# A gated delta rule core: inverse by transposes, modulation sums moved from TensorE to VectorE, pieces reordered

## What is computed

```python
a_mat = jnp.where(strict, bc[..., :, None] * kk * decay, 0.0) + jnp.eye(CHUNK)
rhs = jnp.concatenate([vc * bc[..., None], kc * (bc * jnp.exp(gam))[..., None]], axis=-1)
sol = lax.linalg.triangular_solve(a_mat, rhs, left_side=True, lower=True, unit_diagonal=True)
...
mod = (c_act @ ada_w[l] + ada_b[l])[:, None, :]
sh1, sc1, g1, sh2, sc2, g2 = jnp.split(mod, 6, axis=-1)
...
x = x + g1 * hybrid_mixer(h, ...)
```

## Time and profile before

| What | us |
| --- | --- |
| median of the runs | 2159.68 |
| span of the profiled execution | 2156.4 |
| the rest of that time, taken as median less span | 3.3 |
| TensorE busy | 1983.0 (92%) |
| VectorE busy | 511.2 (24%) |
| ScalarE busy | 327.1 (15%) |
| GpSimd busy | 96.9 (4%) |

### The profile page before, as it was taken

The page is one execution under the profiler, slowest core; times in us unless marked ns, Lnnn a source line. Parts: engine busy times, 40 slices in busy tenths (PEclk is TensorE's granted clock), DMA queues, the critical chain, the costliest instruction groups (busy, mean ns, idle before and its releaser), DMA issues. The chain is left out here.

```text
span 2156.4 us, 23922 instructions
## 1 busy us (share of the span) xinstructions
PE 1983.0 (92%) x9874; PEld 954.2 (44%) x9874; DVE 511.2 (24%) x1030; ACT 327.1 (15%) x572; POOL 96.9 (4%) x178
## 2 busy tenths in 40 slices
PE   6989999989999999999999999899999887777777
PEld 4677676643333333333333333355454432223322
DVE  2255453431222122121122111231342300000000
ACT  2133421220000000000000000213341200000001
POOL 2010052000000000000000000100030000000000
PEclk9999999999999999999999999999999998999999
DMA  9332254579999999999999999934243799999996
GB/s 342 117 122 84 73 210 173 206 312 425 428 428 429 429 428 428 428 428 429 428 429 428 429 429 429 394 119 168 63 152 155 287 428 429 428 429 429 428 429 290
DMA packets 98563, 707.10 MB, mean 328 GB/s; under 512 B 12314, under 2 KB 17932, under 8 KB 61516
## 3 DMA queue, kind: packets, MB, share of 16 engines
q1 hardware_dynamic: 98508, 706.36, 79.9%
HBM read 705.29 MB, written 1.05 MB: 328 GB/s over the span
## 5 line engine op out<-in xcount | busy, mean ns | idle before, releaser
L1674 PE MATMUL ps<-ring,arena 128*64 128x512 f32 x1536 | 337.5, 593 | 12.0 <-DMA ring<-in_moe_w_gu 12.0
L2870 PE MATMUL ps<-ring,arena 128*32 128x512 f32 x768 | 175.5, 621 | 41.5 <-DMA ring<-in_w_up 20.4
L1674 PEld LDWEIGHTS ps<-ring,arena 128*64 128x64 f32 x1536 | 109.8, 137 | 234.2 <-issue 206.1
L1701 PE MATMUL ps<-ring,arena 128*64 128x512 f32 x768 | 168.9, 592 | 0.0
L2107 PE MATMUL ps<-ring 128*128 128x512 f32 (+1 forms) x320 | 138.8, 583 | 0.7 <-ACT ring L2486 0.6
L1725 ACT ACTIVATE arena<-arena 128x512 f32<-128x512 f32 x32 | 20.2, 630 | 760.3 <-DVE arena L1756 760.3
L2870 PEld LDWEIGHTS ps<-ring,arena 128*32 128x32 f32 x768 | 52.8, 114 | 163.3 <-issue 161.4
L1674 PE MATMUL ps<-arena 128*64 128x512 f32 x512 | 113.5, 593 | 4.5 <-DMA arena<-in_moe_w_gu 4.5
L1069 PEld LDWEIGHTS ps<-arena 128*128 128x128 f32 x832 | 99.2, 197 | 35.3 <-issue 32.7
L1069 PE MATMUL ps<-arena 128*128 128x128 f32 x832 | 107.2, 285 | 2.3 <-DVE arena L1061 1.3
L1701 PEld LDWEIGHTS ps<-ring,arena 128*64 128x64 f32 x768 | 54.9, 137 | 109.9 <-issue 100.2
(11 more groups left out here) (581 smaller groups left out, 2093.5 us busy)
## 6 DMA issues: line engine op xcount, KB each, us to landing
ring<-in_moe_w_gu SPq DMA_DIRECT2D x96, 2048.0 KB, 28.8
ring<-in_moe_w_down SPq DMA_DIRECT2D x48, 2048.0 KB, 31.6
arena<-in_moe_w_gu SPq DMA_DIRECT2D x32, 2048.0 KB, 28.8
ring<-in_w_up SPq DMA_DIRECT2D x24, 2048.0 KB, 20.1
ring<-in_w_gate SPq DMA_DIRECT2D x24, 2048.0 KB, 26.9
ring<-in_w_down SPq DMA_DIRECT2D x24, 2048.0 KB, 27.0
ring<-in_w_in SPq DMA_DIRECT2D x22, 2048.0 KB, 8.4
arena<-in_moe_w_down SPq DMA_DIRECT2D x16, 2048.0 KB, 33.8
```

What stands on the lines that cost most here:

```text
L1674: last = M.matmul(ps[halves[j], 4 + which, :], xgT[buf][:, k, CAP * ee:CAP * ee + CAP], w[:, k2, at:at + 512], start=False, stop=(k == KD ...
L1701: last = M.matmul(ps[halves[j], 6, :], yT[:, k % KH, halves[k // KH]], w[:, k % KH, 512 * j:512 * j + 512], start=False, stop=(k == 2 * KH ...
L2870: last = M.matmul(ps[quads[e], 4 + which, :], xgT[:, k, quads[e]], w[e][:, k, :], start=(k == 0), stop=(k == KD - 1))
```

## The change

Three things are changed together, all within the 24 steps.

1. The product for Xi (Q1^T Xi) and its subtraction on VectorE are gone. In their place `transposed_back(i)` transposes the updated Yi on TensorE, and ScalarE copies it from PSUM over Xi (`take_transposed`). It comes in the program one step later, after `corrections(i+1)`, for i = 0 to 19; the last of these levels transposes 64 x 64 blocks only. `corrections(i)` now waits for the copy that belongs to step i-4, and each transpose waits for VectorE's update of Yi.
2. The late modulation sums no longer run on TensorE and ScalarE. VectorE forms them with 8 instructions for each of the 8 chunks, 128 x 512 each, which read the weights from the ring slot and one column of the condition as a scalar: one multiplication and seven multiply-adds, each waiting for the one before. Four such instructions follow the update in each of the steps 0 to 3 and three in each of the steps 4 to 19. `s_ada`, which frees the slot, is now raised by VectorE.
3. The pieces beside the steps have other places, and their waits are adapted.

```diff
+    LATE_SUMS = [(j, k) for j in range(4, 12) for k in range(KD)]
+    def late_sums_of(i):
+        at = 4 * i if i < 4 else 16 + 3 * (i - 4)
+        return LATE_SUMS[at:at + (4 if i < 4 else 3)]
...
-    BESIDE = {0: [("mt", 0)], 1: [("sum", 4)], 2: [("spread", 4), ("sum", 5)], 3: [("spread", 5)], 4: [("mt", 1)],
...
+    BESIDE = {0: [("mt", 0)], 1: [("mt", 1)], 2: [("spread", 4)], 4: [("spread", 5)], 5: [("out", 0, 0)], 6: [("out", 0, 1)],
+              7: [("spread", 6)], 8: [("out", 1, 0)], 10: [("spread", 7)], 11: [("out", 1, 1)], 12: [("spread", 8)],
+              15: [("spread", 9)], 18: [("spread", 10)], 20: [("spread", 11)]}
...
+                if i >= 4:
+                    pe.wait_ge(s_yt, 2 + i - 3)
                 for h in range(4 * g, 4 * g + 4):
...
-                if lv < NL - 1:
-                    for h in range(4 * g, 4 * g + 4):
-                        last = M.matmul(ps[:, 4 + i % 2, (h % 4) * P:(h % 4 + 1) * P], Q1[t][:, h, :], Xi[t][:, h, :])
                 last.then_inc(s_dd, 1)
+            def transposed_back(i):
+                lv, t, g = STEPS[i]
+                pe.wait_ge(s_upd, i + 1)
+                if i >= 2:
+                    pe.wait_ge(s_yt, 2 + i - 1)
+                for h in range(4 * g, 4 * g + 4):
+                    if lv < NL - 2:
+                        last = M.transpose(ps[:, 4 + i % 2, (h % 4) * P:(h % 4 + 1) * P], Yi[t][:, h, :], ident[:, :])
+                    else:
+                        last = M.transpose(ps[0:HB, 4 + i % 2, (h % 4) * HB:(h % 4 + 1) * HB], Yi[t][0:HB, h, 0:HB], ident[0:HB, 0:HB])
+                last.then_inc(s_xt, 1)
...
-                elif kind == "sum":
...
-                    modulation_sums(pe, cond, 6)
                 elif kind == "spread":
-                    pe.wait_ge(s_part, j + 1)
-                    if j > 4:
+                    pe.wait_ge(s_ada, j + 1)
+                    if j == 4:
+                        pe.wait_ge(s_mTt, 2)
+                    else:
                         pe.wait_ge(s_modt, j - 4)
...
                     if t == 0:
-                        chunk[n] = ra.take(pe)
+                        chunk[n] = ra.arrived(pe, out_chunk[1, n])
                     pe.wait_ge(s_mTt, 2)
-                    if n:
-                        pe.wait_ge(s_part, 8)
-                        pe.wait_ge(s_modt, 4)
+                    if n and t == 0:
+                        pe.wait_ge(s_wev, 1)
+                    if t:
+                        pe.wait_ge(s_modt, 4 if n else 2)
...
                 corrections(i)
+                if 1 <= i <= NSTEP - 4:
+                    transposed_back(i - 1)
                 for piece in BESIDE.get(i, ()):
                     beside(piece)
...
+            def take_transposed(i):
+                lv, t, g = STEPS[i]
+                act.wait_ge(s_xt, 2 + i + 1)
+                if lv < NL - 2:
+                    A.activation(Xi[t][:, 4 * g:4 * g + 4, :], four(4 + i % 2), ACT.Copy).then_inc(s_yt, 1)
...
-                    elif piece[0] == "sum":
-                        j = piece[1]
-                        act.wait_ge(s_ada, j + 1)
-                        act.wait_ge(s_comb, j - 1)
-                        A.activation(mod_parts[j % 2], ps[:, 6, :], ACT.Copy).then_inc(s_part, 1)
...
+            def late_sum(j, k):
+                acc = mod_parts[j % 2]
+                if k == 0:
+                    late_w[j] = ra.arrived(dve, late_chunk[j])
+                    dve.wait_ge(s_comb, j - 1)
+                    vv(V.tensor_scalar(acc, late_w[j][:, 0, :], cond[:, 0, 0:1], None, ALU.mult))
+                else:
+                    ins = V.scalar_tensor_tensor(acc, late_w[j][:, k, :], cond[:, k, 0:1], acc, ALU.mult, ALU.add)
+                    if k < KD - 1:
+                        vv(ins)
+                    else:
+                        ins.then_inc(s_ada, 1)
...
                 dve.wait_ge(s_dd, i + 1)
-                y, x = Yi[t][:, 4 * g:4 * g + 4, :], Xi[t][:, 4 * g:4 * g + 4, :]
+                y = Yi[t][:, 4 * g:4 * g + 4, :]
                 if lv < NL - 1:
-                    vv(V.tensor_tensor(x, x, four(4 + i % 2), ALU.subtract))
                     V.tensor_tensor(y, y, four(2 + i % 2), ALU.subtract).then_inc(s_upd, 1)
...
+                for j, k in late_sums_of(i):
+                    late_sum(j, k)
```

More of the change, by code:

```diff
@@ L185, in load, with arrived @@
                 self.sent += 1
+        def arrived(self, eng, n):
+            _, (k, w), _, s, arrivals, _ = self.chunks[n]
+            eng.wait_ge(self.full[s], arrivals)
+            return slot(s, k, w)
         def take(self, pe):
-            _, (k, w), _, s, arrivals, _ = self.chunks[self.used]
-            pe.wait_ge(self.full[s], arrivals)
             self.used += 1
-            return slot(s, k, w)
+            return self.arrived(pe, self.used - 1)
     w_in, ada_w = a["w_in"][0], a["ada_w"][0]
@@ L209, in program @@
     s_wout = sem("w_out_chunk_multiplied")
+    late_chunk, out_chunk = {}, {}
     def add_late(j, s):
+        late_chunk[j] = len(ra.chunks)
         ra.add(cols(ada_w, 512 * j), (KD, 512), (s_ada, j + 1), s)
     def add_out(k, n, released, s):
+        out_chunk[k, n] = len(ra.chunks)
         ra.add(a["w_out"][0][1024 * k:1024 * k + 1024, 512 * n:512 * n + 512]
@@ L1081, in program @@
     NSTEP = len(STEPS)
-    BESIDE = {0: [("mt", 0)], 1: [("sum", 4)], 2: [("spread", 4), ("sum", 5)], 3: [("spread", 5)], 4: [("mt", 1)],
-              5: [("out", 0, 0)], 7: [("out", 0, 1)], 8: [("sum", 6)], 9: [("spread", 6), ("sum", 7)], 10: [("spread", 7)],
-              11: [("out", 1, 0)], 13: [("out", 1, 1)], 14: [("sum", 8)], 15: [("spread", 8), ("sum", 9)], 16: [("spread", 9)],
-              17: [("sum", 10)], 18: [("spread", 10), ("sum", 11)], 19: [("spread", 11)]}
+    BESIDE = {0: [("mt", 0)], 1: [("mt", 1)], 2: [("spread", 4)], 4: [("spread", 5)], 5: [("out", 0, 0)], 6: [("out", 0, 1)],
[5 more added lines that the diff above has]
+        return LATE_SUMS[at:at + (4 if i < 4 else 3)]
     def cell(b, h):
@@ L1255, in beside @@
                     last.then_inc(s_mT, 1)
-                elif kind == "sum":
-                    pe.wait_ge(s_mTt, 1 if j < 6 else 2)
-                    pe.wait_ge(s_part, j)
-                    if j >= 6:
-                        pe.wait_ge(s_wev, 1 if j < 8 else 3)
-                    modulation_sums(pe, cond, 6)
                 elif kind == "spread":
-                    pe.wait_ge(s_part, j + 1)
-                    if j > 4:
+                    pe.wait_ge(s_ada, j + 1)
+                    if j == 4:
+                        pe.wait_ge(s_mTt, 2)
+                    else:
                         pe.wait_ge(s_modt, j - 4)
@@ L1295, in _ @@
             pe.wait_ge(s_modt, 8)
-            pe.wait_ge(s_part, 12)
+            pe.wait_ge(s_wev, 4)
             per_head(6, lambda h: (kx[0][:, h, :], Ug[0][:, h, :])).then_inc(s_st, 1)
@@ L1324, in _ @@
             for n in range(2):
-                chunk[n] = ra.take(pe)
+                chunk[n] = ra.arrived(pe, out_chunk[0, n])
                 project(n, 0)
@@ L1410, in _ @@
                     take_product(i + 1)
+                if 1 <= i <= NSTEP - 4:
+                    take_transposed(i - 1)
                 for piece in BESIDE.get(i, ()):
@@ L1493, in take_part @@
                 return V.tensor_tensor(x_res[:, t, at], x_res[:, t, at], wo_t, ALU.add)
+            def late_sum(j, k):
[8 more added lines that the diff above has]
+                        vv(ins)
+                    else:
+                        ins.then_inc(s_ada, 1)
+            late_w = {}
             dve.wait_ge(s_yt, 2)
```

5 lines of the change are left out of this document (3 added, 2 removed).

## The result

The changed kernel takes 2167.3 us (median of four runs, 2167.07 to 2170.09) against 2158.86 us (four runs, 2155.0 to 2160.71) for the kernel before: ratio 1.0043 [1.0031, 1.0055], 8.4 us slower. Five more runs of the changed kernel, against 17 of the one before, gave 1.0047 [1.0033, 1.0061]. Forecast were 2162.7 us: right in direction, 4.6 us short.

What follows compares the result with a forecast made beforehand. TensorE's queue was taken to bound the steps, with VectorE becoming slower after the change. The stretches, 4.9 - 2.2 + 0.7 = +3.4, rounded to 3 us, on 2159.7 gave 2162.7 us, range 2159 to 2166.

Steps and rivals of the forecast that it cites:

- What bounds, and that the expert stage passes the shift on: TensorE's queue bounds the steps, 109.82 of 110 us; the expert stage behind shifts by what the steps gain or lose.
- VectorE becomes the slower engine: In every step without a projection piece VectorE needs 2.7 us, TensorE 2.2 us.
- GpSimd's price: In the steps, GpSimd's products and VectorE's sums alternate: 1.0 us per mask product meeting sums, 2.1 us per wide one.
- rival A: In the steps, VectorE and GpSimd don't hinder one another, or GpSimd gives way: 2147.4 us, chance 0.20.
- The four gaps: TensorE waits some 8 us in two gaps by step 2's spread, 2.2 later, 2.7 and 3.7 by projection pieces.
- I take this one to one: The kernel's time changes by exactly the change in the end of the steps, 398.97 us before.
- the three stretches: Steps to first projection piece's start, 4.9 us later; to fourth's end, 2.2 earlier; to last corner update, 0.7 later.
- The multiply-add: In VectorE's sums, a dependent 128 x 512 multiply-add takes 692 ns plus 0.03 us, so 0.72 us.
- The clock: Half clock for 3.3 us costs 1.65 us each before third and fourth projection pieces, 0.8 for the first two gaps.
- Rival C: Clock falls in short gaps too, before the second spread and in steps 19 to 21: 2167 us, chance 0.20.
- B: The clock does not fall in TensorE's gaps in the steps, giving back 4.1 us: 2158.6 us, chance 0.15.

Runs made afterwards that it cites:

- transposes only: The kernel before with Xi by transposes alone, modulation sums left on TensorE and ScalarE, pieces in their old places: 2153.51 us, ratio 0.9977.
- half of the sums: The changed kernel with only chunks 6 to 9 summed on VectorE, beside the projection pieces, the other four late chunks on TensorE: 2148.28 us, ratio 0.9952.
- the last one: The kernel with four late chunks summed on VectorE and four on TensorE, with third and fourth projection pieces moved one step later: 2143.36 us, ratio 0.9921.
- the fillers: The changed kernel with useless TensorE products before two waits, for the spread of step 2 and the fourth projection piece: 2166.5 us, ratio 1.0035.
- narrow masks: The changed kernel with GpSimd's masks from step 4 on and its four wider products cut to 4 columns per head: 2155.25 us, ratio 0.9986.

## Why the prediction was right in its direction and wrong in its size

Forecast was +3 us against a kernel before of 2159.7. Measured were +8.4: the steps gave 5.4, and everything outside them, put at nothing, the other 3.0. So the forecast had 2.4 us too little for the steps and 3.0 for the rest; the kernel before was 0.8 us faster than taken, which leaves the 4.6 us. Two steps of the prediction failed, and they come last below.

**What bounds, and that the expert stage passes the shift on: right.** The steps grew by 5.4 us and the expert stage kept its 914 us.

**VectorE becomes the slower engine: right.** The transposes alone gained 9.1 us of steps, and the sums took 14.4.

**GpSimd's price: right in kind, and near in size.** The forecast lies 15.3 us above rival A, which leaves this charge out; cutting the masks down gave 11.3 us of steps and 15.1 us of VectorE's time, with the masks of the first four steps left whole. The Trainium skill (SBUF — State Buffer, SBUF: two separate sides) says that the holder of the shared ports fully blocks the other. The rows lie near that: the multiplication took 2.52 − 0.48 = 2.0 us more beside a wide product of 2.37 us. Three multiply-adds beside GpSimd's masks took 4.99 us in place of 2.33, some 0.9 us more each: the two engines take turns by instruction.

**The four gaps: right in place and size.** Forecast about 8 us in two gaps, then 2.2, 2.7 and 3.7; measured 3.31 + 4.39 = 7.7, then 2.20, 2.59 and 3.88. The last sum that the first spread waits for was put 305.7 − 288.41 = 17.3 us behind the start of the steps and came (302.81 + 5.36 = 308.17, less 290.96) at 17.2.

**The first step that failed: "I take this one to one: the answer is the change in the end of the steps".** Everything ahead of and behind the steps was put at nothing, and the stage's unchanged length was the only reason given. There lie about 3 of the 8.4 us, the larger part of what the forecast missed. In the means of the spans it is 4.3 of 9.7 us. Of these, 1.3 is the later start, which two profiles of the kernel before have too and which is perhaps chance; 0.7 is the slower group of products behind the steps, present in all four profiles of the changed kernel; 1.3 comes from the one profile with 316.1 us between the stages. The last 1.0 has no cause shown. The other kernels of this study point the same way: the steps of "transposes only" are 9.1 us shorter and its time is 5.3 us less, those of "half of the sums" 15.2 and 10.5. Only the last one kept nearly all, 17.3 and 15.5. Why the part behind grows by 1.3 to 5.1 us in these six kernels stays open.

**The second step that failed is the sum of the three stretches**, by two terms. In the first profile, against the same marks: first stretch 321.70 − 290.96 = 30.7 against 24.6 before, +6.1 for +4.9; second 372.89 − 321.70 = 51.2 against 54.7, −3.5 for −2.2; third 406.81 − 372.89 = 33.9 against 31.2, +2.7 for +0.7. In sum +5.3 for +3.4, which was rounded down to 3.

1. *The multiply-add, charged at a pitch of 0.72 us by the earlier trace rows.* Its row takes 0.751 and the pitch is 2.33 / 3 = 0.78. The nearest shape was taken as equal, though its scalar is a constant and here it is a column of `cond`; whether that makes the difference no run tells. The error is multiplied: some 0.06 us by 21 in the third stretch is 1.3 of the 2.0 that it missed, and by 7 behind the first spread 0.4 of the 1.2 in the first.
2. *The clock, charged in the wrong places.* Granted clock in stretches of the changed kernel:

```profile
303.00:308.00 5.00, 0.84 (x4) 0.44 (x4) 4.89 (x4) 0.60 (x1) 3.05 (x2) 0.52 0.00 0
308.00:313.50 5.50, 5.27 (x19) 4.24 (x20) 4.11 (x7) 0.60 (x1) 1.27 (x1) 0.50 0.78 258
...
345.70:352.70 7.00, 6.99 (x17) 3.16 (x18) 1.50 (x2) 0.00 (x0) 0.00 (x0) 1.00 0.70 259
364.20:368.20 4.00, 3.95 (x6) 1.67 (x7) 2.67 (x4) 0.00 (x0) 0.00 (x0) 0.57 0.00 0
...
401.60:404.00 2.40, 2.35 (x14) 1.17 (x15) 1.00 (x2) 0.00 (x0) 0.00 (x0) 0.63 0.82 228
```

Behind the two first gaps the clock was at half for some 10 us, not 3.3, and VectorE stood 1.45 us for a correction (the row at 313.69) where 0.8 was charged. Before the third piece, charged 1.65, it did not fall at all: 1.00 behind an idle 2.59 us. Without this charge the forecast of the second stretch would be −3.85, close to the −3.5 measured. Before the fourth the charge was right (8.80 against 7.03 is 1.8). Behind the short gaps at the end, 1.41 and 1.82 us with 0.41 us of work between, it fell, which was charged nothing: the spread and what follows took 403.13 − 401.65 = 1.5 us instead of 0.9. Rival C had this place, but also the 2.2 us gap, behind which the clock stayed at 1.00. B, no fall at all, fails on these rows; its price of 4.1 us was not measured, since the fillers brought other falls.

The measured 2167.3 us is the figure of rival C, 2167, and that is luck: C expected it from the clock in the steps, 3.4 to 5 us above the forecast, and the steps ended 2.4 above it, with the rest outside.

## What to carry to other kernels

An engine with idle time can take over work at no cost only where its idle time lies: the sums of all eight chunks cost 14 us of steps when spread evenly, and those of four chunks nothing when they stood beside the four long products of TensorE, where GpSimd mostly rests too. When a change has two parts, ask for each what it gives alone; here one gained 9 us and the other lost more. Before a VectorE instruction that reads two SBUF tensors is moved, look at what GpSimd does at that time. And code outside the changed stage is not to be put at nothing because it is untouched: here the part behind took 1.3 to 6.9 us more in every profile of every altered kernel.

## What the runs showed of the hardware that was not expected

- The length of a gap alone doesn't tell whether the clock falls behind it. In the changed kernel it stayed at 1.00 behind 2.59 us (third piece) and 2.20 us (second spread), and fell behind 1.41 and 1.82 us at the end of the steps. The gap of 2.20 us before the second spread cost nothing there, where the engine had been at half clock until some 3 us before the gap. It cost the clock in the kernel with fillers (0.51 from 315.1 to 318.6 us), where the engine had run at full clock since 305 us, and so did 2.13 us at this place with narrow masks. But the 2.59 us before the third piece came after 24 us of unbroken work at full clock and cost nothing, so this history alone doesn't sort them either. Filling one gap can move the fall to the next.
- An undisturbed multiply-add of 128x512 with a column as its scalar takes 751 ns; one with a constant as its scalar, L1759, takes 692.
- VectorE's multiply-adds over two SBUF tensors and GpSimd's products take turns instruction by instruction, and the waiting shows as a longer instruction (983 ns in the mean and not 751), not as idle time. A multiplication that reads one SBUF tensor and a column is held up as well: 2.52 us and not 0.48 beside a wide product.
